# Attention of two layers in steps of four units instead of two, with eight score buffers and five buffers for transposed rows

## The reference, cut to what matters

```python
s = q @ k.T * scale + bias          # layer 0: a window of 256 or 384 keys, with a sink logit
                                    # layer 1: a neighbourhood, 192 or 256 keys
                                    # 4 memory heads of each layer: 256 keys, no bias
p = softmax(s)
o = p @ v
```

## Time and profile before

| what | value |
|---|---|
| median of 3 runs | 2431.65 us (2429.78 to 2432.81) |
| profiled execution, time | 2432.14 us |
| its span in the profile | 2429.8 us |
| PE busy | 2329.2 us, 96% of the span |
| DVE busy | 1016.1 us, 42% |
| ACT busy | 877.9 us, 36% |
| mean granted clock of PE | 0.978 |

### The profile page before, as it was taken

The page is one execution under the profiler, slowest core; times in us unless marked ns, Lnnn a source line. Parts: engine busy times, 40 slices in busy tenths (PEclk is TensorE's granted clock), DMA queues, the critical chain, the costliest instruction groups (busy, mean ns, idle before and its releaser), DMA issues.

```text
span 2429.8 us, 41306 instructions
## 1 busy us (share of the span) xinstructions
PE 2329.2 (96%) x17380; PEld 1913.5 (79%) x17380; DVE 1016.1 (42%) x1577; ACT 877.9 (36%) x1445; POOL 1004.8 (41%) x553
## 2 busy tenths in 40 slices
PE   7999999999899999999989999999999999999998
PEld 6867788888786778888867888686888777888886
DVE  6164522211465452221156987266343455322212
ACT  5174432222425442232243232635333244333222
POOL 4423544444542354444464444335000365444443
PEclk9999999999999999999999999989999899999999
DMA  6601333333431123333343333323000322333331
GB/s 172 150 17 53 98 102 96 94 95 98 106 99 36 37 77 96 97 100 91 98 118 91 97 100 107 100 74 114 4 4 4 140 71 80 93 98 101 91 96 66
DMA packets 386314, 210.30 MB, mean 87 GB/s; under 512 B 36928, under 2 KB 378664, under 8 KB 385876
## 3 DMA queue, kind: packets, MB, share of 16 engines
q1 hardware_dynamic: 383011, 196.78, 28.5%
q0 software_dynamic: 2448, 9.70, 1.0%
q10 hardware_dynamic: 672, 1.18, 0.1%
HBM read 196.75 MB, written 12.41 MB: 86 GB/s over the span
## 4 chain that ended last, share of the span: by engine, by line
PE 90%; DVE 3%; ACT 3%; issue 2%; POOL 2%; ACTq 0%; DMA 0%; POOLq 0%; DVEq 0%
PE ps L1958 24%; PE ps L1960 24%; PE ps L1959 24%; PE ps L2371 3%; PE ps L2358 2%; PE ps L2075 2%; PE ps L2336 2%; PE ps L2050 1%; PE ps L2060 1%; POOL x_res L750 1%; POOL w_lo L689 1%; PE ps L1917 1%; PE ps L2385 1%; PE ps L2038 1%; ACT w_hi L858 1%
## 5 line engine op out<-in xcount | busy, mean ns | idle before, releaser
L689 POOL TENSOR_TENSOR w_lo<-raw,w_hi 128x1024 fp32r<-128x1024 f32 (+2 forms) x344 | 811.2, 2359 | 947.7 <-ACT w_hi L858 943.9
L1958 PE MATMUL ps<-h_hi,w_hi 128*128 128x512 f32 x2016 | 802.3, 398 | 30.9 <-ACT h_hi L940 12.9
L1959 PE MATMUL ps<-h_hi,w_lo 128*128 128x512 f32 x2016 | 792.6, 393 | 0.0
L1960 PE MATMUL ps<-h_lo,w_hi 128*128 128x512 f32 x2016 | 792.3, 393 | 0.0
L858 ACT ACTIVATE w_hi<-raw 128x1024 fp32r<-128x1024 f32 (+2 forms) x344 | 356.9, 1038 | 1165.7 <-PE ps L1960 1160.6
L1958 PEld LDWEIGHTS ps<-h_hi,w_hi 128*128 128x128 f32 x2016 | 383.7, 190 | 126.4 <-issue 42.7
L1960 PEld LDWEIGHTS ps<-h_lo,w_hi 128*128 128x128 f32 x2016 | 383.3, 190 | 81.7
L1959 PEld LDWEIGHTS ps<-h_hi,w_lo 128*128 128x128 f32 x2016 | 384.1, 191 | 79.9 <-issue 1.6
L1958 PE MATMUL ps<-hid_hi,w_hi 128*128 128x512 f32 x528 | 205.4, 389 | 0.0
L1959 PE MATMUL ps<-hid_hi,w_lo 128*128 128x512 f32 x528 | 205.4, 389 | 0.0
L1960 PE MATMUL ps<-hid_lo,w_hi 128*128 128x512 f32 x528 | 205.4, 389 | 0.0
(11 more groups left out here) (328 smaller groups left out, 2654.1 us busy)
## 6 DMA issues: line engine op xcount, KB each, us to landing
raw<-in_w_gu SPq DMA_DIRECT2D x88, 512.0 KB, 3.8
raw<-in_w_in SPq DMA_DIRECT2D x56, 512.0 KB, 3.8
raw<-in_w_down SPq DMA_DIRECT2D x32, 448.0 KB, 3.7
raw<-in_ffn_w_gate SPq DMA_DIRECT2D x22, 512.0 KB, 3.8
raw<-in_ffn_w_up SPq DMA_DIRECT2D x22, 512.0 KB, 3.9
raw<-in_w_in_b SPq DMA_DIRECT2D x20, 512.0 KB, 4.4
raw<-in_w_down SPq DMA_DIRECT2D x16, 512.0 KB, 4.1
raw<-in_w_out SPq DMA_DIRECT2D x16, 512.0 KB, 4.0
```

What stands on the lines that cost most here:

```text
L689: nc.gpsimd.tensor_tensor(lo[:, k0:, :], src[:, k0:, :], hi[:, k0:, :].bitcast(f32), ALU.subtract).then_inc(lo_done, 1)
L1958: nc.tensor.matmul(bank, wh[:, k, :], ah[:, 0:width], start=first, stop=False)
L1959: nc.tensor.matmul(bank, wl[:, k, :], ah[:, 0:width], start=False, stop=False)
L1960: return nc.tensor.matmul(bank, wh[:, k, :], al[:, 0:width], start=False, stop=end)
```

## The change

It does four things.

1. The order on PE is now made of steps of four units: scores of units i to i+3 in a row; transposes of units i-4 and i-3; value products of units i-8 and i-7; transposes of units i-2 and i-1; value products of units i-6 and i-5.
2. `SCORE_BUFFERS` goes from 6 to 8, so a score buffer is reused by the unit eight on.
3. `PT_BUFFERS` goes from 6 to 5, so a copy waits for the value product of the unit five back.
4. The `keep_clock` matmuls at the start, 1 and 3 in two places before, are now 4 in one place.

The lists of DVE and ACT keep their order. In them only the semaphore values of the waits follow the buffer numbers.

```diff
-PT_BUFFERS = 6
-SCORE_BUFFERS = 6
+PT_BUFFERS = 5
+SCORE_BUFFERS = 8
 TURN_LAG = 4
...
-                for i in range(0, NU + TURN_LAG + 4, 2):
-                    for k in (i, i + 1):
-                        if k < NU:
-                            scores(k)
-                    if i < 4:
-                        keep_clock(512, (1, 3)[i // 2])
-                    for k in (i - TURN_LAG - 1, i - TURN_LAG):
+                for i in range(0, NU + 2 * TURN_LAG, 4):
+                    for k in range(i, min(i + 4, NU)):
+                        scores(k)
+                    if i == 0:
+                        keep_clock(512, 4)
+                    for k in (i - TURN_LAG, i - TURN_LAG + 2):
                         if 0 <= k < NU:
                             turned(k)
-                    if 0 <= i - TURN_LAG - 4 < NU:
-                        with_values(i - TURN_LAG - 4)
+                            turned(k + 1)
+                        if 0 <= k - 4 < NU:
+                            with_values(k - 4)
                 spread_sums(7)
```

## The result

The changed kernel takes 2445.56 us (median of 5 runs, 2443.69 to 2454.7) against 2431.65 (5 runs, 2429.18 to 2436.74). The medians differ by 13.9 us; forecast were 12. The ratio estimated from all runs is 1.0067, with a 95% interval of 1.005 to 1.0083, which is 16.3 us (12.2 to 20.2).

What follows compares the result with a forecast made beforehand. PE was taken to set the time of the two attention stretches, 152 us. Steps lengthened by 13.3 us, less 0.5 to 1 of present waits, gave +12 on 2432.1: 2444 us, own range 2438 to 2451, stated range 2430 to 2453.

Steps and rivals of the forecast that it cites:

- What PE is spared: Four scores in a row on PE save one fixed part, 0.21 us in each of 26 steps, 5.5 at most.
- What PE waits for: PE's second pair of transposes: transpose i-1 waits for DVE's copy of i-3, behind maxima and copies; steps together +13.3 us.
- steps from 8m+4: Steps of four units beginning at a tile's fifth unit; with normalise +0.79 us layer 0, +1.04 layer 1, memory +0.83.
- layer 0, 8m: Layer 0 step of four units beginning at a tile's first unit: 4.60 us against 4.30, +0.30.
- memory, first step 8m: Memory heads, step beginning at a tile's first unit: transpose at 2.9, step 3.9 us against 3.62, +0.28.
- the five buffers: Layer 0, 8m: copy also waits for the value product of i-8, ending at 2.67; copy begins 2.67 to 2.86 us.
- the normalise: DVE's normalise stands ahead of the copy in 8m+4 steps and adds 0.60 us; the first such step lacks it.
- The ends: The first steps and the last of both layers stay at nothing, between -1 and +1 us.
- The sum: Layer 0 4.85, layer 1 5.65, memory 2.8, together 13.3; present waits -0.5 to -1: +12 us.
- The first (only the saved drains count): Waits vanish behind other work if layer 0's copy of i-3 begins by 2.5 us: 2426 us, chance 0.09.
- The second (steps from 8m gain): Only steps with a normalise wait, ten at +0.85, 16 others at -0.21: 2437 us, chance 0.15.
- The third (the clock): Idle PE lowers the granted clock, a quarter of 26 steps at 1.2 GHz: 2464 us, chance 0.04.

Runs made afterwards that it cites:

- both_outputs_moved: dve_order_pt6 with the last steps of a tile's output on ACT and POOL moved a few units later: 2428.48 us, ratio 0.998 to the kernel before.
- pt6: The changed kernel with six buffers for transposed rows and seven score buffers: 2437.89 us, ratio 1.0039 to the kernel before.
- dve_order_pt6: The changed kernel with maxima, copies and normalise reordered in DVE's list, six transposed-row buffers and seven score buffers: 2434.45 us, ratio 1.0005.

## Why the prediction was right, point by point

**What PE is spared.** Held. Four scores take 1.28 us in layer 0 (forecast 1.27), 0.96 in layer 1 (0.95), 1.06 with memory heads (1.05). The clean steps of both_outputs_moved reach 4.06 where 4.07 was worked out. By the saved fixed parts alone the kernel would be faster, as both_outputs_moved is. The rule of the Trainium skill ("TensorEngine Tiling (Array Packing)", Key Properties), that a change of tiling mode drains the engine, agrees with the 0.20 us that the merged scores save; whether this is the drain or another fixed part of a group, no run here separates.

**What PE waits for.** Held in place and in cause: the second unit of the second pair waits for a copy, in both kinds of steps, and in most steps from 8m+4 the chain runs as forecast through DVE (in that from unit 36, in both layers, its last links are ACT's exponential and copy). A tile takes 10.68 us from 151.59 (forecast 10.6). But the sizes of the terms were off, in both directions ("before" is half a tile as in the prediction, for the memory heads the step measured in each layer):

| step | forecast | measured | before |
|---|---|---|---|
| layer 0, 8m | 4.60 | 4.71 to 4.90, mean 4.81 | 4.30 |
| layer 0, 8m+4 with normalise | 5.09 | 4.96 to 5.23, mean 5.04 | 4.30 |
| layer 0, 8m+4 without | 4.49 | 4.93 | 4.30 |
| layer 1, 8m | 3.85 | 3.95 to 4.23, mean 4.10 | 3.64 |
| layer 1, 8m+4 with normalise | 4.68 | 4.39 to 4.67, mean 4.48 | 3.64 |
| layer 1, 8m+4 without | 4.08 | 4.42 | 3.64 |
| memory, first step 8m | 3.90 | 4.75 and 4.33 | 4.16 and 3.76 |
| memory, 8m+4 | 4.45 | 4.44 and 4.44 | 3.83 and 3.76 |
| memory, second step 8m | 3.90 | 3.91 and 3.91 | 3.62 and 3.62 |

**The term that was too small: the five buffers.** For a step from 8m in layer 0 the sum let the copy of i-3 begin between 2.67 and 2.86 us (the upper bound follows from none of the terms shown). In the trace it begins at 2.97 (154.56 - 151.59). Two parts were left out. The first pair of transposes takes 1.00 us instead of 0.81, since transpose i-3 waits until the copy of i-5 is out of its bank, and the value products behind it end later. And the copy begins 0.09 us after the moment at which PE's next group could start (154.56 against 153.88 + 0.59). Taking the buffer back gave 0.4 to 0.5 us in three of the five steps from 8m in layer 0, where I had allowed 0.2 (expectation of pt6), and 0.34 to 0.49 in all five of layer 1. In the other two of layer 0 (units 8 and 32), where ACT has the copies of i-5 and i-2, nothing changed. There DVE's list sets it: in the step from unit 32 the copy of i-3 begins 2.88 us after the scores with either number of buffers, not at the 2.48 of the sum, as the copy of i-4 ahead of it waits for its own transposes.

**The term that was too large: the normalise.** Forecast as 0.60 in each of ten steps over one without it; in the changed kernel the difference is 4.93 to 5.04, 0.1 us. With six buffers it is 0.33 (4.64 to 4.97), and taking it away gives 0.55. Five buffers lengthen the step without it to nearly the same. In the sum of layer 0, one fewer copy in two of three cases gives a mean of 4.02 us and not 3.98; that is 0.04 us in a step and changes nothing.

**The ends.** Put at nothing, -1 to +1. Measured: start of layer 0 +0.3, of layer 1 -0.2, the last part of each layer +0.7: +1.6. The last part is back to 10.7 with six buffers, in both layers, so this is theirs too.

**The sum.** Forecast for attention +12.3, measured +16.3: the steps made 14.7 instead of 12.5, the ends 1.6. The median moved by 13.9, and the ratio of 1.0067 is 16.3 us. That the difference of the medians lies nearer to the forecast than the stretches do is luck, not insight: single runs of the changed kernel lie up to 11 us apart. It is luck as well that errors of both signs cancelled in part, with layer 0 too low (its steps 5.9 us instead of 4.85) and the steps with a normalise in layer 1 too high.

**The rivals.** The first (only the saved drains count) was refuted with its condition: the copy began at 2.97 us, not by 2.5. The second (steps from 8m gain) fell: they lost 0.5. The third (the clock) fell: 1.00 in both stretches, with waits in every step.

**Not settled.** The eight score buffers and the other placing of `keep_clock` had no run of their own. The traces bound the latter: the start of a layer, where it stands, changed by +0.3 and -0.2 us. Which part of the remaining +1.3 of dve_order_pt6 is POOL's list and which ACT's wasn't separated, since the last experiment moved both.

## What to carry to other kernels

A larger step on one engine saves its fixed parts (here 0.2 us per step) but changes which instructions of the others are due in it. Look at each list that is in order: where the lag of a copy was fitted to the old step, it is now behind work that the new step doesn't need first. A ring of buffers must be counted in steps, not units: here the sixth buffer was worth nothing at two units a step and 8 us at four. And such an edit should be made with its companions: PE's order with five buffers lost 0.6 to 0.7%; with the sixth buffer, DVE's order and the outputs' places changed as well it gained 0.2%.

## What was not expected of the hardware

The granted clock stayed at 1.00 in both stretches though PE waited in nearly every step and was busy only 88% of the time (78.03 of 88.30 us). And a matmul stretch whose code is the same to the last instruction varied more from execution to execution (the rest of the kernel, 2274 to 2287 us) than most of the edits here are worth; only the stretch's own length, which repeats to 0.05 us, could rank them.
